# One projection in a two-block transformer kernel: its matmuls ordered by token block and not by column half, with the normalisation between them

## The chip, the core and the metric

The kernel runs on one core of one Trainium2 chip. The metric is the device time of one execution in microseconds (us), the median of three runs; lower is better.

## The reference, cut to what matters

The whole reference is two residual blocks (forgetting and dilated attention with retention after it, then a block of a state-space mixer beside sliding-window attention and a gated feed-forward part). x has 256 tokens (two blocks of 128) and 1024 channels. The change touches the seam of the second block between its mixing and its feed-forward part:

```
merged = concatenate([rms_norm(y_ssm, g_ssm_out), rms_norm(y_attn, g_attn_out)])   # 256 x (512 + 512)
h  = h + rms_norm(merged @ w_out, g_post_mix)                                      # 256 x 1024
hn = rms_norm(h, g_pre_ffn)
gu = hn @ w_gate_up                                                                # 256 x 5632
ff = (silu(gu[..., :D_FF]) * gu[..., D_FF:]) @ w_down
```

## The kernel before, in words

Each engine has a program of its own, written out in order by hand, and they meet at semaphores. TensorE multiplies in three passes per weight tile (high part of the activation by high part of the weight, low by high, high by low). Activations go to it transposed, in `act_t`: eight tiles of high parts (`x_hi`) and eight of low parts (`x_lo`).

Weights pass through a ring of four slots (`RING = 4`) in units of 128 x 1024 values (512 KB). SP loads a unit into `stage` once the low part of the unit four before it has been made; ScalarE makes the high part `w_hi` (line 627) once TensorE has used the unit four before it (`unit_used`); VectorE makes `w_lo` (line 914). `split_hi(u)` and `split_lo(u)` do this for all units below u that aren't done yet; `ahead(name)` does it to three units past the named chunk.

A chunk is 512 output columns. Its result lies in two PSUM banks, one for each token block; chunks alternate between banks 0, 1 and banks 2, 3. `start_chunk(name)` makes TensorE wait until the chunk before last, which used the same banks, has been drained; the semaphores are counted for even and odd chunks. In number, the chunks around the change are mix_attn 0 (35), glu 1 (36), glu 0 (37), mix_attn 1 (38), mix_ssm 0 (39), mix_ssm 1 (40), ffn 0 (41). I call the four units of mix_ssm U0, U1 (columns 0 to 511) and U2, U3 (columns 512 to 1023), and those of ffn 0 U4 to U7, those of ffn 1 U8 to U11. mix_attn and mix_ssm are the halves of `merged @ w_out` for the attention and the state-space part. mix_attn 1 is drained by ScalarE in `take_attn_half(1)` (line 846, two copies from PSUM into `mixed`), which stands behind the split of the transposed `ssm_out` (line 654) and its squares (line 643).

TensorE after mix_attn 1: it transposes `ssm_out` (line 1440), multiplies mix_ssm 0 for both blocks (lines 1508 to 1516), then mix_ssm 1, all of block 0 first and then block 1 (lines 1882 to 1887), runs small matmuls on a matrix of ones that only keep it busy (`keep_busy`, line 1574), and transposes x block by block (line 1898). Then the feed-forward chunks begin (lines 1548 and 1552).

VectorE adds the PSUM result to `mixed` (`mix_sum(c, b)`, line 1351), ScalarE squares it (line 868), VectorE multiplies it with the gain in place (`mix_gain`, line 1356), sums the squares of a block (`mix_mean`, line 1362), GpSimd raises that to the power -1/2 (line 597), VectorE updates x (`x_add(c, b)`, line 1367). TensorE transposes x, ScalarE makes the high parts (line 654, from PSUM, 256 tokens at once), VectorE the low parts (line 951).

Of the kernel before, what the change touches and what calls it, by code (L numbers as in the profile page):

```python
# [26 lines left out]
P = 128  # L27
# [105 lines left out]
def build(nc, t):  # L133
# [4 lines left out]
    with ExitStack() as ctx:  # L138
# [122 lines left out]
        x_ready, h_ready, mix_gained = sem("x_ready"), sem("h_ready"), sem("mix_gained")  # L261
# [356 lines left out]
        def _(act):  # L618
# [11 lines left out]
            def ahead(name):  # L630
                split_hi(last_unit[name] + 1 + AHEAD)
# [228 lines left out]
            hi_of_turned(3 * KD + 20, 4, 4, COL_GSSM)  # L860
            squares(5, lambda b: ssm_out[:, b, :], lambda b: gate_z[:, b, :])
            take_attn_half(1)
            ahead(("mix_ssm", 0))
            for c in range(2):
                for b in range(NB):
                    act.wait_ge(mixed_ready, 2 * c + b + 1)
                    half = slice(c * 512, (c + 1) * 512)
                    nc.scalar.activation(junk[:, b, half], mixed[:, b, half], ACT.Square, scale=D**-0.5, accum_out=(sumsq, sumsq_b)[c][:, 12 + b:13 + b]).then_inc(squared, 1)
# [36 lines left out]
        def _(dve):  # L905
            next_unit = [0]

            def split_lo(until):

                for u in range(next_unit[0], min(until, n_units)):  # L910
                    if u in lower_by_pool:
                        continue
                    dve.wait_ge(hi_ready, u + 1)
                    nc.vector.tensor_tensor(w_lo[:, u % RING, :], stage[:, u % RING, :], w_hi[:, u % RING, :].bitcast(F32), ALU.subtract).then_inc(lo_ready, 1)  # L914
                next_unit[0] = max(next_unit[0], min(until, n_units))

            def ahead(name):
                split_lo(last_unit[name] + 1 + AHEAD)
# [430 lines left out]
            def mix_sum(c, b):  # L1349

                STT(mixed[:, b, halves[c]], result(("mix_ssm", c))[:, b, :], rstd[:, 10 + b:11 + b], mixed[:, b, halves[c]], ALU.mult, ALU.add).then_inc(mixed_ready, 1)

            def mix_gain(c, b):

                dve.wait_ge(squared, squared_count(5) + 2 * c + b + 1)
                return TT(mixed[:, b, halves[c]], mixed[:, b, halves[c]], row_a[:, halves[c]], ALU.mult)

            def mix_mean(b):

                dve.wait_ge(squared, squared_count(5) + 2 + b + 1)  # L1360
                c = slice(12 + b, 13 + b)
                STT(sumsq[:, c], sumsq[:, c], EPS, sumsq_b[:, c], ALU.add, ALU.add).then_inc(block_mean, 1)

            def x_add(c, b):

                dve.wait_ge(rstd_ready, 7 + b)
                STT(x[:, b, halves[c]], mixed[:, b, halves[c]], rstd[:, 12 + b:13 + b], x[:, b, halves[c]], ALU.mult, ALU.add).then_inc(x_ready, 1)

            ahead(("mix_ssm", 0))
            chunk_drained(dve, ("mix_attn", 0))  # L1370
            chunk_done(dve, ("mix_ssm", 0))
            for b in range(NB):
                mix_sum(0, b)
            mix_gain(0, 0)
            mix_gain(0, 1).then_inc(drain_sem(("mix_ssm", 0)), 1)
            chunk_drained(dve, ("mix_attn", 1))
            dve.wait_ge(mix_block, 1)
            mix_sum(1, 0)
            mix_gain(1, 0).then_inc(mix_gained, 1)
            mix_mean(0)  # L1380
            chunk_done(dve, ("mix_ssm", 1))
            mix_sum(1, 1)
            chunk_drained(dve, ("mix_ssm", 0))
            dve.wait_ge(mix_gained, 1)
            x_add(0, 0)
            mix_mean(1)
            x_add(1, 0)
            mix_gain(1, 1).then_inc(drain_sem(("mix_ssm", 1)), 1)
            chunk_drained(dve, ("mix_ssm", 1))
            x_add(0, 1)  # L1390
            x_add(1, 1)
            lo_of_turned(3 * KD + 24, 4, 0, COL_FFN, KD)
            split_lo(next_unit[0] + 1)
            lo_of_turned(3 * KD + 28, 4, 4, COL_FFN + 4, KD + 4)
# [37 lines left out]
        def _(pe):  # L1432
# [59 lines left out]
            def lower_there(name, j):  # L1492

                wait_lower(pe, chunks[name][0] + j)
# [74 lines left out]
            def after_lo(count):  # L1569
                return lambda k: pe.wait_ge(act_hi, count + k + 1), lambda k: pe.wait_ge(act_lo, count + k + 1)  # L1570
# [302 lines left out]
            name = ("mix_ssm", 1)  # L1873
            start_chunk(name)
            for b in range(NB):
                tok = slice(b * P, (b + 1) * P)
                out = result(name)[:, b, :]
                for j in range(2):
                    hi, lo = unit_of(name, j)
                    for i in range(2):  # L1880
                        k = 2 * j + i
                        mm(out, x_hi(4 + k)[:, tok], hi[:, i, :], start=(k == 0), stop=False)
                        mm(out, x_lo(4 + k)[:, tok], hi[:, i, :], start=False, stop=False)
                    lower_there(name, j)
                    for i in range(2):
                        k = 2 * j + i
                        ins = mm(out, x_hi(4 + k)[:, tok], lo[:, i, :], start=False, stop=(k == CT - 1))
                    if b == 1:
                        ins.then_inc(unit_used, 1)
                if b == 0:  # L1890
                    ins.then_inc(mix_block, 1)
            for b in range(NB):
                keep_busy((6, 3)[b], (7, 0)[b])
                for k in range(KD):
                    if k % 4 == 0:
                        pe.wait_ge(x_ready, 2 * b + k // 4 + 1)
                    o = 4 * BANK + k * S + b * P
                    ins = nc.tensor.transpose(ps[:, o:o + P], x[:, b, k * P:(k + 1) * P], ident[:])
                    if b == 1:
                        ins.then_inc(turned, 1)  # L1900
            for c in range(11):
                start_chunk(("ffn", c))
                if c == 0:
# [63 lines left out]
```

## Time and profile before

| | |
|---|---|
| median of 3 runs | 798.84 us (797.82 to 799.75) |
| profiled execution, its own time | 795.62 us |
| its span, first to last instruction | 793.8 us |
| TensorE busy | 776.1 us, 98% of the span |
| VectorE, ScalarE, GpSimd busy | 513.3, 405.3, 232.8 us |
| mean granted TensorE clock | 0.996 |
| moved by DMA | 130.72 MB, 165 GB/s |

Times below are microseconds from the start of the span. A row of the timeline gives the start and the length of a run of like instructions, the engine, the source line, what is written and read, the shape and the count; in brackets stands how long the engine sat idle before it, and what ended that. PEld is the weight load of TensorE, PE its matmul. The granted clock is given as a share of 2.4 GHz.

### The profile page before, as it was taken

To read this page: it belongs to the slowest core of one execution; us is meant where nothing else is said; L and a number is where in the kernel's file an instruction comes from. 1 tells how busy PE (TensorE), PEld (TensorE's weight loads), DVE (VectorE), ACT (ScalarE), POOL (GpSimd) and SP (SyncE) were. 2 spreads that over 40 slices of the span, in tenths; PEclk is the share of its full clock that TensorE was granted. 3 is DMA by queue.
4 is the path that set the end of the run, shared out by engine and by line. 5 is a ranking of instruction groups with operands and counts; after the bars stand their busy time and mean duration, and the time that the engine had idled before them with its cause. 6 is when DMAs were issued, how large, how long until landed. Compare 5 with 4: busy or idle time off the path is not lost.

```text
span 793.8 us, 12695 instructions
## 1 busy us (share of the span) xinstructions
PE 776.1 (98%) x5133; PEld 679.3 (86%) x5133; DVE 513.3 (65%) x753; ACT 405.3 (51%) x649; POOL 232.8 (29%) x186
## 2 busy tenths in 40 slices
PE   7999999999999999999999999998999999999996
PEld 6889988999888889987778888987887888888885
DVE  4756864764547657865557965766678776777453
ACT  5754436534565545344335545717766555556341
POOL 3031895570742000036009910126002111011010
PEclk9999999999999999999999999999999999999999
DMA  8997895387721554654545556430363656655651
GB/s 218 213 266 217 208 207 150 82 193 170 167 81 51 187 173 147 213 171 147 158 136 158 179 195 185 135 132 2 119 220 127 199 186 210 187 176 172 220 177 54
DMA packets 77821, 130.72 MB, mean 165 GB/s; under 512 B 4414, under 2 KB 28210, under 8 KB 77634
## 3 DMA queue, kind: packets, MB, share of 16 engines
q1 hardware_dynamic: 76418, 125.00, 54.4%
q0 software_dynamic: 1200, 4.83, 1.9%
q8 instruction: 41, 0.67, 0.3%
q14 instruction: 18, 0.15, 0.1%
q10 hardware_dynamic: 144, 0.07, 0.0%
HBM read 128.82 MB, written 1.06 MB: 164 GB/s over the span
## 4 chain that ended last, share of the span: by engine, by line
PE 94%; DVE 2%; ACT 2%; issue 1%; DMA 1%; POOL 0%; DVEq 0%; SPq 0%; POOLq 0%; ACTq 0%
PE ps L1508 15%; PE ps L1516 15%; PE ps L1512 15%; PE ps L1548 10%; PE ps L1527 6%; PE ps L1531 6%; PE ps L1535 6%; PE ps L1552 5%; PE ps L1615 2%; PE ps L1634 2%; PE ps L1647 1%; PE ps L1646 1%; PE ps L1645 1%; PE ps L1925 1%; PE ps L1790 1%
## 5 line engine op out<-in xcount | busy, mean ns | idle before, releaser
L914 DVE TENSOR_TENSOR w_lo<-stage,w_hi 128x1024 fp32r<-128x1024 f32 x226 | 296.1, 1329 | 164.8 <-ACT w_hi L627 164.4
L627 ACT ACTIVATE w_hi<-stage 128x1024 fp32r<-128x1024 f32 x232 | 242.5, 1061 | 237.1 <-PE ps L1516 116.8
L1508 PE MATMUL ps<-w_hi,act_t 128*128 128x512 f32 (+1 forms) x376 | 102.5, 396 | 3.1 <-issue 2.6
L1516 PE MATMUL ps<-w_lo,act_t 128*128 128x512 f32 (+1 forms) x376 | 99.6, 388 | 1.0 <-issue 1.0
L1548 PE MATMUL ps<-act_t,w_hi 128*128 128x512 f32 x352 | 88.3, 393 | 0.7 <-DVE act_t L951 0.7
L1508 PEld LDWEIGHTS ps<-w_hi,act_t 128*128 128x128 f32 x376 | 68.4, 189 | 18.5 <-issue 5.7
L1516 PEld LDWEIGHTS ps<-w_lo,act_t 128*128 128x128 f32 x376 | 70.2, 190 | 15.7 <-issue 1.2
L1512 PE MATMUL ps<-w_hi,act_t 128*128 128x512 f32 (+1 forms) x312 | 82.3, 387 | 0.0
L1548 PEld LDWEIGHTS ps<-act_t,w_hi 128*128 128x128 f32 x352 | 63.3, 189 | 12.1 <-issue 0.9
L1512 PEld LDWEIGHTS ps<-w_hi,act_t 128*128 128x128 f32 x312 | 58.0, 189 | 12.0
L1527 PE MATMUL ps<-act_t,w_hi 128*128 128x256 f32 x416 | 58.8, 284 | 0.0
L1531 PE MATMUL ps<-act_t,w_hi 128*128 128x256 f32 x416 | 58.4, 283 | 0.0
L1535 PE MATMUL ps<-act_t,w_lo 128*128 128x256 f32 x416 | 58.4, 283 | 0.0
L1527 PEld LDWEIGHTS ps<-act_t,w_hi 128*128 128x128 f32 x416 | 53.8, 193 | 0.2
L1535 PEld LDWEIGHTS ps<-act_t,w_lo 128*128 128x128 f32 x416 | 53.7, 193 | 0.0
L1531 PEld LDWEIGHTS ps<-act_t,w_hi 128*128 128x128 f32 x416 | 53.7, 193 | 0.0
L1552 PEld LDWEIGHTS ps<-act_t,w_lo 128*128 128x128 f32 x352 | 48.0, 190 | 3.4
L1552 PE MATMUL ps<-act_t,w_lo 128*128 128x256 f32 x352 | 49.1, 283 | 0.0
L604 POOL TENSOR_TENSOR big<-big 128x512 f32<-128x512 f32 x11 | 14.3, 1300 | 105.5 <-ACT big L884 105.5
L1512 PE MATMUL ps<-w_hi,y_lo 128*128 128x512 f32 x128 | 34.3, 390 | 0.0
L1512 PEld LDWEIGHTS ps<-w_hi,y_lo 128*128 128x128 f32 x128 | 24.1, 188 | 5.1
L433 POOL TENSOR_TENSOR sumsq<-sumsq,sumsq_b 128x2 f32<-128x2 f32 x2 | 0.4, 194 | 91.0 <-ACT junk L643 91.0
(364 smaller groups left out, 1195.4 us busy)
## 6 DMA issues: line engine op xcount, KB each, us to landing
stage<-in_even_w_in SPq DMA_DIRECT2D x64, 512.0 KB, 5.7
stage<-in_odd_w_in SPq DMA_DIRECT2D x48, 512.0 KB, 4.2
stage<-in_w_gate_up SPq DMA_DIRECT2D x44, 512.0 KB, 4.6
stage<-in_w_down SPq DMA_DIRECT2D x22, 512.0 KB, 4.5
stage<-in_even_w_out SPq DMA_DIRECT2D x16, 512.0 KB, 4.3
stage<-in_odd_w_out SPq DMA_DIRECT2D x16, 512.0 KB, 4.1
stage<-in_w_in SPq DMA_DIRECT2D x10, 512.0 KB, 3.7
stage<-in_w_out SPq DMA_DIRECT2D x8, 512.0 KB, 4.9
```

The costliest lines, as they stand in the source:

```text
L627: nc.scalar.activation(w_hi[:, u % RING, :], stage[:, u % RING, :], ACT.Copy).then_inc(hi_ready, 1)
L914: nc.vector.tensor_tensor(w_lo[:, u % RING, :], stage[:, u % RING, :], w_hi[:, u % RING, :].bitcast(F32), ALU.subtract).then_inc(lo_ready, 1)
L1508: mm(out[:, b, :], a_hi(k)[:, tok[b]], hi[:, i, :], start=(k == 0), stop=False)
L1512: mm(out[:, b, :], a_lo(k)[:, tok[b]], hi[:, i, :], start=False, stop=False)
L1516: ins = mm(out[:, b, :], a_hi(k)[:, tok[b]], lo[:, i, :], start=False, stop=(k == k_tiles - 1))
L1527: mm(out[m], columns(hi[:, i, :], m), act_t[:, k, :], start=(k == 0 and m % 2 == 0), stop=False, skip_group_check=True)
L1531: mm(out[m], columns(hi[:, i, :], m), act_t[:, KD + k, :], start=False, stop=False, skip_group_check=True)
L1535: ins = mm(out[m], columns(lo[:, i, :], m), act_t[:, k, :], start=False, stop=(k == k_tiles - 1), skip_group_check=True)
L1548: mm(out[m], hi[:, i, w[m]], both[:, :, k, :], start=(k == 0), stop=(k == KD - 1), skip_group_check=True)
L1552: ins = mm(out[m][:, 0, :], lo[:, i, w[m]], act_t[:, k, :], start=False, stop=(k == KD - 1), skip_group_check=True)
L1615: even = mm(bank(0, width, at), qs[0][:, tok], ks[0][:, 0:width], start=True, stop=True)
L1634: ins = nc.tensor.transpose(bank(2 + n % 2, P, part * P), prob[:, n % 3, part * P:(part + 1) * P], ident[:])
```

## The change

mix_ssm 0 and mix_ssm 1 are no longer one after the other. TensorE calls `start_chunk` for both, then multiplies block 0 with U0, U1, U2, U3, and then block 1 with the same four. Before the last unit of block 1 it transposes block 0 of x (`turn_block(0)`). The gained halves go into `ssm_out` and `gate_z` and not back into `mixed`, so `mix_gain` waits for the sum alone and not for the squares. ScalarE and VectorE make the high and low parts of x for one block at a time (128 tokens, eight tiles each), block 0 with semaphores of its own. The splits of the weight units U3 to U5 are given new places. `keep_busy` is called once, with 9 matmuls, before block 1 of x is transposed; before, it was called with 6 ahead of block 0 and with 3 ahead of block 1. (In the trace each of these matmuls leaves two records, so 6 of them are a row with x12.)

```diff
@@ scalar engine
-            ahead(("mix_ssm", 0))
-            for c in range(2):
-                for b in range(NB):
-                    act.wait_ge(mixed_ready, 2 * c + b + 1)
-                    ...
+            split_hi(last_unit[("mix_ssm", 1)] + 1)
+            def hi_of_block(b, made):
+                for k in range(KD):
+                    act.wait_ge(x_turned, KD * b + (k | 1) + 1)
+                    o = 4 * BANK + k * S + b * P
+                    nc.scalar.activation(act_t[:, k, b * P:(b + 1) * P], ps[:, o:o + P], ACT.Copy, scale=col[:, COL_FFN + k:COL_FFN + k + 1]).then_inc(made, 1)
+            mix_squares(0, 0)
+            mix_squares(1, 0)
+            mix_squares(0, 1)
+            split_hi(last_unit[("mix_ssm", 1)] + 3)
+            hi_of_block(0, first_hi)
+            mix_squares(1, 1)
+            hi_of_block(1, act_hi)
             ahead(("mix_ssm", 1))
-            hi_of_turned(3 * KD + 24, KD, 0, COL_FFN)
@@ vector engine
             def mix_gain(c, b):
-                dve.wait_ge(squared, squared_count(5) + 2 * c + b + 1)
-                return TT(mixed[:, b, halves[c]], mixed[:, b, halves[c]], row_a[:, halves[c]], ALU.mult)
+                dve.wait_ge(mixed_ready, 2 * b + c + 1)
+                TT(gained[c][:, b, :], mixed[:, b, halves[c]], row_a[:, halves[c]], ALU.mult).then_inc(drain_sem(("mix_ssm", c)) if b == 1 else mix_gained, 1)
...
+            split_lo(last_unit[("mix_ssm", 1)] + 1)
+            for c in range(2):
+                chunk_drained(dve, ("mix_attn", c))
+                dve.wait_ge(mix_block, c + 1)
+                mix_sum(c, 0)
+                mix_gain(c, 0)
+            mix_mean(0)
             chunk_done(dve, ("mix_ssm", 0))
...
+            mix_sum(0, 1)
+            mix_gain(0, 1)
+            x_add(0, 0)
+            x_add(1, 0)
+            split_lo(last_unit[("mix_ssm", 1)] + 2)
+            lo_of_block(0, first_hi, 0, first_lo)
             chunk_done(dve, ("mix_ssm", 1))
             mix_sum(1, 1)
...
+            mix_gain(1, 1)
             mix_mean(1)
...
+            split_lo(last_unit[("mix_ssm", 1)] + 3)
             x_add(0, 1)
             x_add(1, 1)
...
+            lo_of_block(1, act_hi, 3 * KD + 24, act_lo)
             split_lo(last_unit[("ffn", 0)] + 1)
@@ tensor engine
-            mix_part("mix_ssm", 0, 4, after_lo(3 * KD + 20))
...
+            for c in range(2):
+                start_chunk(("mix_ssm", c))
+            hi_there, lo_there = after_lo(3 * KD + 20)
+            for b in range(NB):
+                tok = slice(b * P, (b + 1) * P)
+                for c in range(2):
+                    name = ("mix_ssm", c)
+                    out = result(name)[:, b, :]
+                    for j in range(2):
...
+                        if b == 1:
+                            ins.then_inc(unit_used, 1)
+                        if (b, c, j) == (1, 1, 0):
+                            turn_block(0)
+                    if b == 0:
+                        ins.then_inc(mix_block, 1)
+            chunk_drained(pe, ("mix_ssm", 0))
+            keep_busy(9, number[("mix_ssm", 0)] % 2 * 2)
+            pe.wait_ge(first_lo, KD)
+            turn_block(1)
```

## Rows read from the trace of the kernel before

**Rows 1.** The page, part 1: busy time, share of the span, instructions.

```profile
PE 776.1 (98%) x5133; PEld 679.3 (86%) x5133; DVE 513.3 (65%) x753; ACT 405.3 (51%) x649; POOL 232.8 (29%) x186
```

**Rows 2.** Windows: PE, PEld, DVE, ACT, POOL busy, clock, DMA share, GB/s.

```profile
640.00:700.00 60.00, 60.00 (x347) 52.96 (x346) 43.45 (x44) 33.85 (x44) 7.80 (x6) 1.00 0.59 182
```

**Rows 3.** Timeline of TensorE around the two mix_ssm chunks.

```profile
585.59 1.03 PE L1440 MATMUL ps<-ident,ssm_out 128*128 128x128 f32 x8
...
586.84 1.16 PE L1508 MATMUL ps<-w_hi,act_t 128*128 128x512 f32 x4 [0.22 <-ACT act_t L654]
...
597.36 0.62 PE L1887 MATMUL ps<-w_lo,act_t 128*128 128x512 f32 x2
597.82 1.50 PE L1574 MATMUL ps<-ones 128*128 128x128 f32 x12
600.22 1.39 PE L1898 MATMUL ps<-ident,x 128*128 128x128 f32 x8 [0.91 <-DVE x L1367]
...
602.34 1.32 PE L1898 MATMUL ps<-ident,x 128*128 128x128 f32 x8
604.32 2.08 PE L1548 MATMUL ps<-act_t,w_hi 128*128 128x512 f32 x8 [0.66 <-DVE act_t L951]
```

**Rows 4.** Timeline of VectorE, ScalarE and GpSimd, 598 to 604 us.

```profile
598.54 0.74 DVE L1351 SCALAR_TENSOR_TENSOR mixed<-ps,rstd,mixed 128x512 f32<-128x512 f32 x1
...
599.32 0.63 ACT L868 ACTIVATE junk<-mixed 128x512 f32<-128x512 f32 x1 [1.49 <-DVE mixed L1351]
...
600.08 0.15 DVE L1362 SCALAR_TENSOR_TENSOR sumsq<-sumsq,sumsq_b 128x1 f32<-128x1 f32 x1
...
600.32 0.99 POOL L597 TENSOR_TENSOR rstd<-sumsq,neg_half 128x1 f32<-128x1 f32 x1 [1.03 <-DVE sumsq L1362]
600.82 0.68 DVE L1356 TENSOR_TENSOR mixed<-mixed,row_a 128x512 f32<-128x512 f32 x1
...
601.53 1.42 DVE L1367 SCALAR_TENSOR_TENSOR x<-mixed,rstd,x 128x512 f32<-128x512 f32 x2
...
602.82 3.03 ACT L654 ACTIVATE act_t<-ps,col 128x256 fp32r<-128x256 f32 x8 [0.88 <-PE ps L1898]
...
603.69 1.66 DVE L951 SCALAR_TENSOR_TENSOR act_t<-ps,col,act_t 128x256 fp32r<-128x256 f32 x4 [0.74 <-ACT act_t L654]
```

**Rows 5.** Timeline of ScalarE, 586 to 590 us.

```profile
586.22 1.57 ACT L654 ACTIVATE act_t<-ps,col 128x256 fp32r<-128x256 f32 x4 [2.04 <-PE ps L1440]
587.66 0.65 ACT L643 ACTIVATE gate_z<-ssm_out 128x512 f32<-128x512 f32 x1
...
588.89 1.27 ACT L846 ACTIVATE mixed<-ps,rstd 128x512 f32<-128x512 f32 x2
```

**Rows 6.** Groups by line, shapes apart: busy us, mean ns of one.

```profile
L818 ACT ACTIVATE qkv<-ps,rstd_in 128x128 f32<-128x128 f32 x2 | 0.7, 368 | 0.0
```

**Rows 7.** Timeline of GpSimd and VectorE: short GpSimd operations and weight splits.

```profile
589.09 0.19 POOL L434 TENSOR_SCALAR rstd<-sumsq 128x2 f32<-128x2 f32 x1 [22.14 <-ACT gate_z L643]
...
598.71 0.57 POOL L597 TENSOR_TENSOR rstd<-sumsq,neg_half 128x1 f32<-128x1 f32 x1 [8.08 <-DVE sumsq L1362]
...
607.97 2.35 DVE L914 TENSOR_TENSOR w_lo<-stage,w_hi 128x1024 fp32r<-128x1024 f32 x2
608.01 2.36 POOL L434 TENSOR_SCALAR rstd<-sumsq 128x2 f32<-128x2 f32 x1 [6.70 <-ACT junk L643]
```

**Rows 8.** Timeline of TensorE at the start of the kernel.

```profile
11.09 1.17 PE L1508 MATMUL ps<-w_hi,act_t 128*128 128x512 f32 x4 [2.63 <-issue]
...
17.33 1.07 PE L1516 MATMUL ps<-w_lo,act_t 128*128 128x512 f32 x4
```

**Rows 9.** Windows there, columns as in rows 2.

```profile
12.00:13.00 1.00, 1.00 (x5) 0.76 (x4) 1.00 (x4) 1.00 (x3) 0.00 (x0) 0.61 0.71 274
...
14.00:15.00 1.00, 1.00 (x4) 0.71 (x4) 1.00 (x4) 1.00 (x3) 0.00 (x0) 0.50 1.01 205
15.00:16.00 1.00, 1.00 (x5) 0.82 (x4) 1.00 (x3) 1.00 (x4) 0.00 (x0) 0.69 1.13 207
```

**Rows 10.** The page, part 6: DMA issues, KB each, us to landing.

```profile
stage<-in_w_gate_up SPq DMA_DIRECT2D x44, 512.0 KB, 4.6
```

More of the change, by code:

```diff
@@ L260, in build @@
         turned, act_hi, act_lo = sem("turned"), sem("act_hi"), sem("act_lo")
-        x_ready, h_ready, mix_gained = sem("x_ready"), sem("h_ready"), sem("mix_gained")
+        x_ready, x_turned, h_ready, mix_gained, first_hi, first_lo = (sem(n) for n in ("x_ready", "x_turned", "h_ready", "mix_gained", "first_hi", "first_lo"))
         dve_step, act_step, pool_step = sem("dve_step"), sem("act_step"), sem("pool_step")
@@ L862, in _, with mix_squares @@
             take_attn_half(1)
-            ahead(("mix_ssm", 0))
-            for c in range(2):
-                for b in range(NB):
-                    act.wait_ge(mixed_ready, 2 * c + b + 1)
-                    half = slice(c * 512, (c + 1) * 512)
-                    nc.scalar.activation(junk[:, b, half], mixed[:, b, half], ACT.Square, scale=D**-0.5, accum_out=(sumsq, sumsq_b)[c][:, 12 + b:13 + b]).then_inc(squared, 1)
+            split_hi(last_unit[("mix_ssm", 1)] + 1)
+            def mix_squares(c, b):
+                act.wait_ge(mixed_ready, 2 * b + c + 1)
+                half = slice(c * 512, (c + 1) * 512)
+                nc.scalar.activation(junk[:, b, half], mixed[:, b, half], ACT.Square, scale=D**-0.5, accum_out=(sumsq, sumsq_b)[c][:, 12 + b:13 + b]).then_inc(squared, 1)
+            def hi_of_block(b, made):
[10 more added lines that the diff above has]
+            hi_of_block(1, act_hi)
             ahead(("mix_ssm", 1))
-            hi_of_turned(3 * KD + 24, KD, 0, COL_FFN)
             act.wait_ge(x_ready, 2 * NB)
@@ L1351, in mix_sum @@
                 STT(mixed[:, b, halves[c]], result(("mix_ssm", c))[:, b, :], rstd[:, 10 + b:11 + b], mixed[:, b, halves[c]], ALU.mult, ALU.add).then_inc(mixed_ready, 1)
+            gained = (ssm_out, gate_z)
             def mix_gain(c, b):
-                dve.wait_ge(squared, squared_count(5) + 2 * c + b + 1)
-                return TT(mixed[:, b, halves[c]], mixed[:, b, halves[c]], row_a[:, halves[c]], ALU.mult)
+                dve.wait_ge(mixed_ready, 2 * b + c + 1)
+                TT(gained[c][:, b, :], mixed[:, b, halves[c]], row_a[:, halves[c]], ALU.mult).then_inc(drain_sem(("mix_ssm", c)) if b == 1 else mix_gained, 1)
             def mix_mean(b):
-                dve.wait_ge(squared, squared_count(5) + 2 + b + 1)
+                dve.wait_ge(squared, squared_count(5) + 2 * b + 2)
                 c = slice(12 + b, 13 + b)
@@ L1366, in x_add @@
                 dve.wait_ge(rstd_ready, 7 + b)
-                STT(x[:, b, halves[c]], mixed[:, b, halves[c]], rstd[:, 12 + b:13 + b], x[:, b, halves[c]], ALU.mult, ALU.add).then_inc(x_ready, 1)
-            ahead(("mix_ssm", 0))
-            chunk_drained(dve, ("mix_attn", 0))
-            chunk_done(dve, ("mix_ssm", 0))
[L1372 to L1380, printed above, removed]
+                if b == 1:
+                    chunk_drained(dve, ("mix_ssm", c))
+                else:
+                    dve.wait_ge(mix_gained, c + 1)
+                STT(x[:, b, halves[c]], gained[c][:, b, :], rstd[:, 12 + b:13 + b], x[:, b, halves[c]], ALU.mult, ALU.add).then_inc(x_ready, 1)
+            def lo_of_block(b, hi_made, n_hi, made):
+                for k in range(KD):
+                    dve.wait_ge(hi_made, n_hi + (k | 1) + 1)
+                    o, tok = 4 * BANK + k * S + b * P, slice(b * P, (b + 1) * P)
+                    STT(act_t[:, KD + k, tok], ps[:, o:o + P], col[:, COL_FFN + k:COL_FFN + k + 1], act_t[:, k, tok].bitcast(F32), ALU.mult, ALU.subtract).then_inc(made, 1)
@@ L1381, in _ @@
             chunk_done(dve, ("mix_ssm", 1))
             mix_sum(1, 1)
-            chunk_drained(dve, ("mix_ssm", 0))
-            dve.wait_ge(mix_gained, 1)
-            x_add(0, 0)
+            mix_gain(1, 1)
             mix_mean(1)
-            x_add(1, 0)
-            mix_gain(1, 1).then_inc(drain_sem(("mix_ssm", 1)), 1)
-            chunk_drained(dve, ("mix_ssm", 1))
+            split_lo(last_unit[("mix_ssm", 1)] + 3)
             x_add(0, 1)
             x_add(1, 1)
-            lo_of_turned(3 * KD + 24, 4, 0, COL_FFN, KD)
@@ L1393, in _ @@
-            split_lo(next_unit[0] + 1)
-            lo_of_turned(3 * KD + 28, 4, 4, COL_FFN + 4, KD + 4)
+            lo_of_block(1, act_hi, 3 * KD + 24, act_lo)
             split_lo(last_unit[("ffn", 0)] + 1)
@@ L1871, in _, with turn_block @@
             turn_rows(lambda b, k: ssm_out[:, b, k * P:(k + 1) * P], 4, 4)
-            mix_part("mix_ssm", 0, 4, after_lo(3 * KD + 20))
[L1873 to L1893, printed above, removed]
+            def turn_block(b):
                 for k in range(KD):
@@ L1897, in _ @@
                     o = 4 * BANK + k * S + b * P
-                    ins = nc.tensor.transpose(ps[:, o:o + P], x[:, b, k * P:(k + 1) * P], ident[:])
-                    if b == 1:
-                        ins.then_inc(turned, 1)
+                    nc.tensor.transpose(ps[:, o:o + P], x[:, b, k * P:(k + 1) * P], ident[:]).then_inc(x_turned, 1)
+            for c in range(2):
[7 more added lines that the diff above has]
+                    for j in range(2):
+                        hi, lo = unit_of(name, j)
+                        for k in range(2 * j, 2 * j + 2):
+                            hi_there(k)
+                            mm(out, x_hi(4 + k)[:, tok], hi[:, k % 2, :], start=(k == 0), stop=False)
+                        for k in range(2 * j, 2 * j + 2):
+                            lo_there(k)
+                            mm(out, x_lo(4 + k)[:, tok], hi[:, k % 2, :], start=False, stop=False)
+                        lower_there(name, j)
+                        for k in range(2 * j, 2 * j + 2):
+                            ins = mm(out, x_hi(4 + k)[:, tok], lo[:, k % 2, :], start=False, stop=(k == CT - 1))
+                        if b == 1:
+                            ins.then_inc(unit_used, 1)
[7 more added lines that the diff above has]
+            turn_block(1)
             for c in range(11):
```

## The prediction

> **What bounds the kernel now.** I read the page first: TensorE is busy for 776.1 of 793.8 us [rows 1], so only its order and its waits can matter. The windows say how strictly: from 640 to 700 us it is busy 60.00 of 60.00 us, at clock 1.00 [rows 2]. Whatever delays the first feed-forward matmul delays the end by as much; no slack behind it could swallow a loss. The question is thus when that matmul (line 1548) starts: at 604.32 us now [rows 3].
>
> The timeline of TensorE gives the seam. The matmuls of mix_ssm start at 586.84 and end at 597.36 + 0.62 = 597.98 [rows 3]. They are 48, and the last pair is issued by about 597.6, so they run one per 0.227 us. From 597.98 to 604.32, 6.34 us, TensorE does only transposes and matmuls on ones [rows 3]. What sets this tail is the dependent chain on the other engines [rows 4]: sum 598.54, square 599.32, mean 600.08, power 600.32 to 601.31, `x_add` 601.53, transposes 602.34, high parts 602.82, low parts 603.69, matmul 604.32. The change wants most of block 0's part of this to lie beside the matmuls.
>
> **The wait that the new order puts in front.** I go through the edit with the before trace as time axis; nothing changes up to the transposes of `ssm_out` (585.59 to 586.62 [rows 3]). Now `start_chunk` of mix_ssm 1 (number 40) stands ahead of all of the 48 matmuls. It waits until all even chunks before it, mix_attn 1 (38) among them, have been drained. That is ScalarE's work at line 846: 588.89 + 1.27 = 590.16 [rows 5], behind four high parts (586.22) and the two squares (from 587.66). ScalarE's order up to there is not edited. Before, TensorE reached this wait after the 24 matmuls of mix_ssm 0, 586.84 + 24 x 0.227 = 592.3, when it was long over: those matmuls were its cover, and the cover is gone. Queued behind the wait are all 48 matmuls, and all of VectorE's sums. First matmul: 590.16 plus the 0.14 us that lies between 604.18, the end of the first low part, and 604.32 [rows 3, 4] (low part taken as 0.49), so 590.3. **Cost 3.45 us.** It is read from code and two rows, so I give it 0.3 us of play.
>
> **Block 0.** Matmuls 1 to 12 are issued by 593.0, 24 by 595.7. Its column 0 is summed under the matmuls. Column 1: the last matmul is over at 595.9, sum to 596.65, square and its read to 597.4 (0.76 us from start of square to start of mean, 599.32 to 600.08 [rows 4]), mean 597.45, power 597.7 to 598.25 (0.57 with VectorE quiet [rows 7]). But VectorE works in order, and ahead of `x_add(0, 0)` stand `mix_sum(0, 1)` and `mix_gain(0, 1)`. The sum waits for U1 used by block 1: 36 matmuls, 590.3 + 35 x 0.227 + 0.39 (the length of one, 0.62 for two less 0.23) = 598.6. Then sum 598.65 to 599.4, gain (0.68) to 600.1, two `x_add` at 0.75 and spacing 0.67 [rows 4], ready at 600.85 and 601.5. TensorE has issued its 42 matmuls at 599.8 and waits for block 0 until 600.9, transposes four tiles, waits again until 601.55, transposes four, and goes on at 602.05. Eight transposes without a wait take about 1.0 us (1.03 [rows 3]); here they take 2.25, **1.25 us of it waiting, 1.0 work** that before lay in the tail. The last six matmuls end at 603.6. That is 597.98 + 3.45 + 2.25, or 603.65.
>
> **Block 1, the new tail.** ScalarE squares `mixed(0, 1)` by 600.2, splits U4 and U5 (about 1.0 us each, the weight copies are on its queue now ahead of the activations) to 602.2, and starts on the high parts of block 0. A 128 x 128 copy from PSUM takes 0.368 [rows 6]; eight of 128 x 256 take 3.03, 0.37 apart [rows 4]. 128 tokens fewer save some 0.10 each (bounds: 0.37, no saving, and half, 0.19); I take 0.27, so the last is done at 604.4. VectorE splits U4 (1.2) from 601.45 to 602.65, then follows ScalarE's pairs; a low part of 256 costs 0.39 apiece (1.66 for four), half as wide I take 0.26. Last low part of block 0 at 605.0. Only behind it stands `mix_sum(1, 1)`, though its matmuls ended at 603.6: **1.35 us of queueing**. From there: sum 605.0 to 605.75, square, mean at 606.5, power issued at 606.7.
>
> Behind the mean, VectorE splits U5, 606.6 to 607.8 (1.2, half of 2.35 [rows 7]), and `x_add(0, 1)` stands behind that. If the power were done in 0.57 to 0.99 [rows 4, 7] the split would just cover it: `x_add` at 607.75. But the power starts inside the split. In rows 7 a GpSimd operation that takes 0.19 elsewhere takes 2.36 us, 608.01 to 610.37, when two splits run on VectorE from 607.97 to 610.32: it ends as they do. So I let the power run after the split, 607.8 + 0.57, and `x_add(0, 1)` at 608.4. The Trainium skill, SBUF — State Buffer, "SBUF: two separate sides", states this as a rule: GpSimd and VectorE share a pair of ports, an instruction of VectorE with two inputs in SBUF holds it for its whole length, and the other blocks fully. By that rule the sum is +6.5, without it +5.9; the trace's 2.36 us agrees with it.
>
> `x_add(0, 1)` to first matmul: before 604.32 - 601.53 = 2.79 [rows 4]; half-wide tiles save two times 0.1 on ScalarE and 0.13 on VectorE, so 2.4. **First feed-forward matmul at 610.8, against 604.32: +6.5 us.** The nine matmuls on ones take 2.2 us (1.50 for six [rows 3]) from 603.5 and are over at 605.7, well before block 1; they cost nothing. Block 1's later tiles arrive 0.3 us apart against 0.46 us for two matmuls, no cost. The ring: U8 is now loaded when U4's low part is done (602.65) and lands in 4.6 us [rows 10], at 607.3; it is needed four units after 610.8, each longer than its eight 512-wide matmuls at 0.227, so not before 618.1. U9, loaded at 607.8, lands at 612.4. No cost. The reciprocal row for the feed-forward part needs squares of x, which follow U6's split: some 3.6 us from first matmul to squares done before, about the same now, and the row is used after three units. No cost, up to 0.4 if it is late.
>
> **The clock.** At the start of the kernel TensorE idles 2.63 us before 11.09 [rows 8], and then the granted clock goes to 0.61, 0.50, and back through 0.69 in the sixteenth us [rows 9]: from the level of 2.4 GHz to that of 1.2 and back. The 24 matmuls from 11.09 to the four at 17.33 show the price: 20 issued in 6.24 us, not 20 x 0.227 = 4.54, a loss of 1.7. In the changed kernel the wait in front is 3.5 us of idling (586.8 to 590.3), longer than that one, and the second, from 605.7 to the transposes at 609.1, 3.4 us, is too. Before, the longest hole here is 0.91 [rows 3]. So I expect a slow stretch twice. How much of it lies on matmuls depends on where it falls: between 0 and 1.7 each; I take 1.3 for the first (all of block 0 hangs on those matmuls) and 0.9 for the second (transposes and waits take part of it). **+2.2 us.** The Trainium skill, TensorE: Matmul & The Clock Gate, "What's actually happening", says that the throttled state is the default and that activity releases it; rows 9 agree.
>
> **Sum**: 3.45 (front) + 2.25 (block 0 in the stream) + 0.8 (tail: 610.8 - 603.65 = 7.15 against 6.34) = 6.5, + 2.2 clock = **+8.7 us**. The profiled execution would be 795.62 + 8.7 = 804.3; the median of the runs shown is 798.84, so 807.5.
>
> **The rivals.**
> - Forecast, both holes lower the clock: 0.50. +7.5 to +10.
> - No slow stretch, or only one: the clock survives, because the hole is bracketed by dense matmuls or falls luckily. For it: holes of 1 us change nothing here. Against it: 2.63 us sufficed once. +6.5, or +7.5 to +8 with one: 0.38.
> - The front wait is hidden: ScalarE drains mix_attn 1 before TensorE asks. It would take the two copies 3.45 us earlier, ahead of the squares and parts. +3.0, and with the clock of the second hole +4: 0.04.
> - The other side, faster: TensorE finds every semaphore of the seam raised, the overlap as drawn. It decides only if the banks are free by 586.8 and x of block 0 by the time of the 42nd matmul. Then 48 matmuls (10.9) and eight transposes (1.0) end at 598.8, and the shortest tail is sum 0.75, square to mean 0.76, mean and power 0.8, `x_add` to matmul 2.4, with gaps 4.9: 603.7, **-0.6 us**, 798.2. Against it: 590.16 [rows 5]. 0.03.
> - The tail is worse than counted (a late row, GpSimd held longer, a slow stretch twice as long as at the start): +10 to +12.5: 0.05.
>
> **How the numbers follow.** Measurements of this kernel tell about 0.2%, 1.6 us, from no change. All cases but the fourth are slower by more than that: slower 0.95; -0.6 us counts as same, and something that I don't see could add to it: same 0.03, faster 0.02. Range: down to +5.2, the case without slow stretches with 1.3 us less in my queueing sums (front 0.3, tile widths 0.4, power not held 0.6), 804.0; up to +12.2: two whole slow stretches (3.4), the late row (0.4), the same 1.3 of queueing sums on the other side, and the power held 0.6 longer, 811.0.
>
> **What would show it.** In the changed profile: TensorE idle 3.5 us before the first mix_ssm matmul, released by ScalarE line 846; a wait of about 1.1 us for `x_add` before block 0's transposes; `mix_sum(1, 1)` starting right after the eighth low part of block 0; the second power over 1 us long and ending after U5's split; clock below 1.00 near 590 to 594 and 609 to 614; the first feed-forward matmul 6.5 to 9 us later in the span, and all later stages as long as before. I am wrong if the front wait is short, if the clock stays at 1.00 (then +6.5), or if the feed-forward part holds slack after all.

## The result: 8 us slower, and the profile after

| | before | changed |
|---|---|---|
| median | 798.64 us (4 runs, 797.82 to 799.75) | 806.66 us (4 runs, 806.02 to 808.36) |
| ratio | | 1.0123, 95% interval 1.0097 to 1.0149 |
| profiled execution, span, mean clock | 795.62, 793.8, 0.996 | 808.36, 806.6, 0.989 |

807.5 was forecast, in a range of 804.0 to 811.0. The two spans differ by 12.8 us, more than the medians. 3.9 us of that arose before the edit: the transposes of `ssm_out` start at 585.59 [rows 3] before and at 589.44 after, and the timeline of the changed kernel's TensorE shows where: a wait of 4.05 us at 59 us, with slow matmuls behind it, which the profiled execution of the kernel before did not have. It ends when VectorE has made the low part of the forget-gate weights, which stands behind the split of a weight unit that came late from DMA. The edit doesn't touch this part, and waits of 1.3 to 4.3 us stand there in all but one of the profiles below. (The kernel before varied from 794.3 to 803.0 us over the runs of this study, so single executions differ by that much without an edit.) I therefore count every time from the start of those transposes, called T0.

Timeline of TensorE in the changed kernel, which answers to rows 3:

```profile
59.24 0.58 PE L1620 MATMUL ps<-act_t,wf_hi 128*128 128x256 f32 x1 [4.05 <-DVE wf_lo L1057]
...
589.44 1.03 PE L1464 MATMUL ps<-ident,ssm_out 128*128 128x128 f32 x8
594.11 0.89 PE L1916 MATMUL ps<-w_hi,act_t 128*128 128x512 f32 x2 [3.64 <-ACT mixed L846]
...
604.87 0.61 PE L1922 MATMUL ps<-w_lo,act_t 128*128 128x512 f32 x2
606.36 1.32 PE L1902 MATMUL ps<-ident,x 128*128 128x128 f32 x8 [0.87 <-DVE x L1388]
...
608.45 0.62 PE L1922 MATMUL ps<-w_lo,act_t 128*128 128x512 f32 x2
608.91 2.17 PE L1598 MATMUL ps<-ones 128*128 128x128 f32 x18
614.36 1.68 PE L1902 MATMUL ps<-ident,x 128*128 128x128 f32 x8 [3.29 <-DVE x L1388]
615.97 3.20 PE L1572 MATMUL ps<-act_t,w_hi 128*128 128x512 f32 x8
```

Read the brackets: 3.64 us of idling in front, ended by ScalarE's copy out of mix_attn 1's banks (line 846), 0.87 for x of block 0, 3.29 for x of block 1. T0 to the first feed-forward matmul is 615.97 - 589.44 = 26.53 us, against 604.32 - 585.59 = 18.73: +7.8. Its first eight matmuls then take 3.20 us and not 2.08 [rows 3]: +1.1. The windows show the clock:

```profile
592.00:594.00 2.00, 0.00 (x0) 0.00 (x0) 0.60 (x2) 2.00 (x7) 0.97 (x3) 1.00 0.77 264
594.00:596.00 2.00, 1.89 (x5) 1.59 (x6) 0.91 (x1) 0.96 (x2) 0.48 (x1) 0.61 0.40 102
596.00:598.00 2.00, 2.00 (x6) 1.55 (x5) 0.31 (x1) 0.00 (x0) 0.00 (x0) 0.53 0.72 215
...
614.00:616.00 2.00, 1.64 (x9) 1.20 (x9) 1.41 (x5) 1.19 (x5) 0.00 (x0) 0.73 0.77 260
616.00:618.00 2.00, 2.00 (x6) 1.63 (x6) 1.67 (x8) 2.00 (x6) 0.00 (x0) 0.50 0.01 3
...
640.00:700.00 60.00, 60.00 (x344) 52.72 (x343) 43.42 (x45) 34.91 (x45) 7.81 (x6) 1.00 0.61 188
```

The clock is the third number from the right: 0.50 is the level of 1.2 GHz. After each long hole the clock falls to it and comes back; in the first hole (592 to 594 us) it was still 1.00. From 640 to 700 us TensorE is busy without a gap, as in rows 2, and the 3.85 us from before T0 and the 8.90 us of the seam (table below) together are the whole difference of the spans, so the seam's loss goes through to the end.

Timelines of VectorE and GpSimd in the changed kernel, which answer to rows 4 and 7:

```profile
604.16 0.75 DVE L1366 SCALAR_TENSOR_TENSOR mixed<-ps,rstd,mixed 128x512 f32<-128x512 f32 x1 [0.95 <-PE ps L1922]
...
608.11 2.16 DVE L1395 SCALAR_TENSOR_TENSOR act_t<-ps,col,act_t 128x128 fp32r<-128x128 f32 x8
610.19 0.74 DVE L1366 SCALAR_TENSOR_TENSOR mixed<-ps,rstd,mixed 128x512 f32<-128x512 f32 x1
...
611.80 1.22 DVE L929 TENSOR_TENSOR w_lo<-stage,w_hi 128x1024 fp32r<-128x1024 f32 x1
613.47 0.75 DVE L1388 SCALAR_TENSOR_TENSOR x<-ssm_out,rstd,x 128x512 f32<-128x512 f32 x1 [0.45 <-POOL rstd L597]
```

```profile
603.30 0.57 POOL L597 TENSOR_TENSOR rstd<-sumsq,neg_half 128x1 f32<-128x1 f32 x1 [8.82 <-DVE sumsq L1379]
611.96 1.47 POOL L597 TENSOR_TENSOR rstd<-sumsq,neg_half 128x1 f32<-128x1 f32 x1 [8.09 <-DVE sumsq L1379]
```

The last `mix_sum` starts at 610.19, right behind the eighth low part of block 0, though its matmuls were over at 609.07. The second power takes 1.47 us, and begins 0.16 us into U5's split.

### The profile page after: what moved, and what is told of

Same layout as the page of the kernel before. It is cut to its first block, busy times and chain, and to the rows that moved or that the text cites. A ratio compares the mean times of both kernels' runs of the same rounds, so it can differ in the third digit from the quotient of the medians.

```text
span 806.6 us, 12720 instructions
## 1 busy us (share of the span) xinstructions
PE 782.3 (97%) x5133; PEld 684.6 (85%) x5133; DVE 515.1 (64%) x761; ACT 406.6 (50%) x657; POOL 230.8 (29%) x186
## 4 chain that ended last, share of the span: by engine, by line
PE 89%; DMA 4%; DVE 3%; ACT 3%; issue 1%; POOL 0%; SPq 0%; DVEq 0%; POOLq 0%; ACTq 0%
PE ps L1532 13%; PE ps L1540 13%; PE ps L1536 13%; PE ps L1572 10%; PE ps L1551 6%; PE ps L1555 6%; PE ps L1559 6%; PE ps L1576 5%; DMA stage<-in_even_w_in 4%; PE ps L1639 2%; PE ps L1658 2%; PE ps L1671 1%; PE ps L1670 1%; PE ps L1669 1%; PE ps L1957 1%; ACT w_hi L627 1%
## 5 line engine op out<-in xcount | busy, mean ns | idle before, releaser
L1532 PE MATMUL ps<-w_hi,act_t 128*128 128x512 f32 (+1 forms) x368 | 100.2, 395 | 0.5 <-ACT act_t L654 0.3
L1540 PE MATMUL ps<-w_lo,act_t 128*128 128x512 f32 (+1 forms) x368 | 96.6, 385 | 0.0
L1540 PEld LDWEIGHTS ps<-w_lo,act_t 128*128 128x128 f32 x368 | 68.1, 188 | 14.1
L1532 PEld LDWEIGHTS ps<-w_hi,act_t 128*128 128x128 f32 x368 | 66.6, 188 | 15.5 <-issue 3.0
L1536 PE MATMUL ps<-w_hi,act_t 128*128 128x512 f32 (+1 forms) x304 | 79.4, 384 | 0.0
L1536 PEld LDWEIGHTS ps<-w_hi,act_t 128*128 128x128 f32 x304 | 56.1, 188 | 11.6
```

Source lines behind the costliest of these rows:

```text
L1532: mm(out[:, b, :], a_hi(k)[:, tok[b]], hi[:, i, :], start=(k == 0), stop=False)
L1536: mm(out[:, b, :], a_lo(k)[:, tok[b]], hi[:, i, :], start=False, stop=False)
L1540: ins = mm(out[:, b, :], a_hi(k)[:, tok[b]], lo[:, i, :], start=False, stop=(k == k_tiles - 1))
```

## The experiments

All kernels start from the changed one and carry one or two edits, the mended ones several. Times are medians; "seam" is T0 to the start of the second feed-forward unit in the profiled execution, which holds both the waits and the slow matmuls of the first unit (before: 607.19 - 585.59 = 21.60 us).

| kernel | median, us | ratio to before, 95% interval | T0 to first feed-forward matmul | seam, over before |
|---|---|---|---|---|
| changed | 806.66 | 1.0123 (1.0097 to 1.0149) | 26.53 | 30.50, +8.9 |
| changed, run again | 807.93 | 1.0122 (1.0097 to 1.0146) | 27.71 | 32.11, +10.5 |
| bank wait late | 803.98 | 1.0076 (1.0052 to 1.0100) | 22.25 | 26.11, +4.5 |
| front hole filled | 805.86 | 1.0103 (1.0079 to 1.0128) | 24.93 | 29.37, +7.8 |
| second hole filled | 805.19 | 1.0096 (1.0074 to 1.0118) | 27.72 | 30.59, +9.0 |
| both filled | 804.18 | 1.0081 (1.0057 to 1.0105) | 24.92 | 27.80, +6.2 |
| U5's low part later | 806.74 | 1.0111 (1.0087 to 1.0135) | 26.63 | 29.50, +7.9 |
| x of block 0 first | 809.55 | 1.0152 (1.0125 to 1.0179) | 27.84 | 32.56, +11.0 |
| x first, copies early | 806.98 | 1.0114 (1.0088 to 1.0141) | 26.47 | 30.95, +9.4 |
| mended | 800.85 | 1.0035 (1.0014 to 1.0056) | 20.21 | 24.38, +2.8 |
| mended, filled | 799.37 | 1.0019 (0.9996 to 1.0041) | 19.92 | 22.80, +1.2 |

The seam's excess and the medians' excess over 798.0 to 798.6 agree within 1.5 us in most rows and within 2.1 in all, so the seam holds the cause, and nothing ahead of T0 adds to the medians. The intervals are some 2 us wide to each side; steps of less than that are judged by the trace, of which there is one for each kernel.

**The changed kernel again.**

> The changed kernel itself, as a yardstick for the runs beside it. Both theories: +8 us against the kernel before (between +7 and +9.5), with a hole of about 3.6 us ahead of the first mix_ssm matmul, one of about 3.3 us ahead of block 1's transposes, and slow matmuls behind each.

The holes are there, 3.64 and 3.29 us, with slow matmuls behind each; the medians differ by 9.7 us, just above the expected range. Timeline and one window of its TensorE:

```profile
588.72 1.19 PE L1916 MATMUL ps<-w_hi,act_t 128*128 128x512 f32 x2 [3.64 <-ACT mixed L846]
...
602.14 1.32 PE L1902 MATMUL ps<-ident,x 128*128 128x128 f32 x8 [0.87 <-DVE x L1388]
...
611.75 3.61 PE L1572 MATMUL ps<-act_t,w_hi 128*128 128x512 f32 x8 [0.38 <-DVE act_t L1395]
```

```profile
588.00:590.00 2.00, 1.28 (x3) 1.13 (x4) 0.30 (x1) 1.56 (x3) 1.09 (x2) 0.50 0.39 119
```

Its slow stretch at the front was the longer one: from the first mix_ssm matmul to the transposes of x it takes 602.14 - 588.72 = 13.42 us, against 606.36 - 594.11 = 12.25 in the first profile. Here the clock was at 0.50 when the matmuls began; in the first profile it fell behind the first of them.

**Bank wait late.**

```diff
-            for c in range(2):
-                start_chunk(("mix_ssm", c))
+            start_chunk(("mix_ssm", 0))
...
                     name = ("mix_ssm", c)
+                    if (b, c) == (0, 1):
+                        start_chunk(name)
```

> TensorE asks for the banks of mix_ssm 1 only before it first writes them, 12 matmuls later. My theory (the bank wait in front costs 3.45 us, and the hole it leaves costs up to 1.7 more through the clock): hole 3.6 us gone, a wait of about 0.7 us behind the 12th matmul in its place, no slow stretch at the front; 4 to 5 us faster than the changed kernel, +3 to +4 over the one before. Rival (the loss sits in the queueing on VectorE and in the tail, the front hole only moves a wait that would come at block 0's x anyway): less than 2 us faster than the changed kernel.

The hole of 3.64 us is gone. Timeline of its TensorE:

```profile
588.44 1.03 PE L1464 MATMUL ps<-ident,ssm_out 128*128 128x128 f32 x8
589.70 0.77 PE L1917 MATMUL ps<-w_hi,act_t 128*128 128x512 f32 x2 [0.22 <-ACT act_t L654]
...
601.08 1.32 PE L1902 MATMUL ps<-ident,x 128*128 128x128 f32 x8 [0.87 <-DVE x L1388]
...
609.08 1.69 PE L1902 MATMUL ps<-ident,x 128*128 128x128 f32 x8 [3.29 <-DVE x L1388]
610.69 3.07 PE L1572 MATMUL ps<-act_t,w_hi 128*128 128x512 f32 x8
```

T0 to first feed-forward matmul falls by 4.3 us against the first profile of the changed kernel, 5.5 against the second; the medians by 2.7 and 4.0. That is less than the 4 to 5 us expected, and +5.7 us over the kernel before, not +3 to +4. The kernel with both holes filled, below, has this wait and no slow clock, and its first feed-forward matmul comes 24.92 us after T0: against it the late bank wait gives 2.7 us. The first mix_ssm matmul comes 3.4 us earlier, and 0.7 us are lost again among the next ones, mostly to waits for low parts. The rest of the gain is the slow clock at the front. The slow stretch behind the second hole is still there. The later bank wait is hardly visible, since the first matmuls wait a little for low parts. What the rival held, that a front wait only moves to block 0's x, is wrong: the wait there is 0.87 us as before, so the whole chain moved with the front.

**Front hole filled, second hole filled, both filled.** Order and waits stay; TensorE does matmuls on ones while it waits.

```diff
             start_chunk(("mix_ssm", 0))
+            keep_busy(13, number[("mix_ssm", 0)] % 2 * 2)
             start_chunk(("mix_ssm", 1))
...
-            keep_busy(9, number[("mix_ssm", 0)] % 2 * 2)
+            keep_busy(20, number[("mix_ssm", 0)] % 2 * 2)
```

> Between the two bank waits stand 13 matmuls on ones (26 records, about 3.2 us), the order and the wait stay. My theory (the front hole lowers the clock): slow stretch at the front gone, matmuls there 0.227 us apart, 1.3 to 1.7 us faster than the changed kernel. Rival (the slow stretch has nothing to do with the hole, or its loss is absorbed by the wait for block 0's x): same time as the changed kernel within 0.5 us.

> keep_busy of 20 and not 9 ahead of block 1's transposes, which fills the second hole (3.3 us) to some 0.6 us. My theory: slow stretch behind the first feed-forward matmul gone, 0.7 to 1.5 us faster than the changed kernel. Rival (that hole is harmless on average, since transposes and waits take the slow stretch): within 0.5 us of the changed kernel.

> The changed kernel with both holes filled with matmuls on ones (13 in front, 20 and not 9 at the second). My theory: no slow stretch in the seam; what is left against the kernel before is waiting and queueing alone, +5.5 to +6.5 us, so 2 to 3.5 us faster than the changed kernel. Rival (the clock costs little): +7.5 us or more.

Timeline of TensorE with both filled:

```profile
588.50 3.07 PE L1598 MATMUL ps<-ones 128*128 128x128 f32 x26
592.25 0.73 PE L1917 MATMUL ps<-w_hi,act_t 128*128 128x512 f32 x2 [0.69 <-ACT mixed L846]
...
602.94 1.32 PE L1902 MATMUL ps<-ident,x 128*128 128x128 f32 x8 [0.88 <-DVE x L1388]
605.48 4.62 PE L1598 MATMUL ps<-ones 128*128 128x128 f32 x40
610.94 1.23 PE L1902 MATMUL ps<-ident,x 128*128 128x128 f32 x8 [0.83 <-DVE x L1388]
612.54 2.08 PE L1572 MATMUL ps<-act_t,w_hi 128*128 128x512 f32 x8 [0.37 <-DVE act_t L1395]
```

The first matmul of mix_ssm comes 4.63 us after T0 (592.25 - 587.62), as late as in the changed kernel (4.67): nothing about the wait has changed. But from there to the transposes of x it is 10.69 us, not 12.25 or 13.42: the slow clock cost 1.6 and 2.7 us in those two executions. The first feed-forward unit takes 2.08 for its eight wide matmuls, not 3.20. Both filled: 2.5 to 3.7 us faster than the changed kernel by the medians, as expected. The front alone gave 0.8 to 2.1 us by the medians, the second hole alone 1.5 to 2.7. In the traces each filling took away its own slow stretch and left the other: with the front filled 10.69 us (603.95 - 593.26) and then 3.57 for the eight wide matmuls, with the second filled 13.43 (603.05 - 589.62) and then 2.08. What stays, 6.2 us in seam and median alike, is waiting and queueing. The two holes' effect on the clock is shown: filling them left the order and the waits as they were.

**U5's low part later.** Without this call, U5's low part is made by the next `split_lo`, behind block 1's low parts.

```diff
             mix_mean(1)
-            split_lo(last_unit[("mix_ssm", 1)] + 3)
             x_add(0, 1)
             x_add(1, 1)
             lo_of_block(1, act_hi, 3 * KD + 24, act_lo)
```

> Against the changed kernel only the low part of unit U5 moves on VectorE, from behind the mean of block 1 to behind the low parts of block 1. My theory (GpSimd's power of block 1 is held by that split, which has two inputs in SBUF): the second power takes 0.57 to 0.7 us and not 1.47, the x update of block 1 starts 0.8 to 0.9 us earlier, 0.7 to 0.9 us faster than the changed kernel, in the trace of the seam if not beyond the spread of the times. Rival (the power is long for another reason, as that it runs right behind an idle spell, and only the split in front of the x update counts): the power stays at 1.47 and the update starts at the power's end as before.

GpSimd's row is what it was made for:

```profile
602.10 0.57 POOL L597 TENSOR_TENSOR rstd<-sumsq,neg_half 128x1 f32<-128x1 f32 x1 [9.83 <-DVE sumsq L1379]
610.76 0.55 POOL L597 TENSOR_TENSOR rstd<-sumsq,neg_half 128x1 f32<-128x1 f32 x1 [8.09 <-DVE sumsq L1379]
```

0.55 and not 1.47, with the same idle spell of 8.09 us in front, so the rival falls. Mean to x update: 611.35 - 610.52 = 0.83 us, against 613.47 - 611.72 = 1.75. T0 to first feed-forward matmul is 1.1 us less than in the kernel run again: these 0.9 us, and 0.2 from a slightly shorter first stretch (13.25 us). The second hole shrank to 2.38 us, and in this profile no slow stretch stands behind it. In the medians, 1.2 us under the kernel run again and 0.1 above the first series, the gain is within the spread.

**x of block 0 first.**

```diff
+            x_add(0, 0)
+            x_add(1, 0)
             chunk_done(dve, ("mix_ssm", 0))
             mix_sum(0, 1)
             mix_gain(0, 1)
-            x_add(0, 0)
-            x_add(1, 0)
```

> Against the changed kernel the two x updates of block 0 stand ahead of the sum and the gain of column half 0 of block 1 on VectorE. My theory (the wait of TensorE ahead of block 0's transposes is queueing on VectorE, not the length of block 0's chain): hole of 0.87 us and the second small one gone, last mix_ssm matmul some 1.1 us earlier; 0.8 to 1.2 us faster than the changed kernel. Rival (the chain of block 0 itself, power included, ends too late): hole stays over 0.5 us.

A miss: the hole went away, and the kernel got slower. Timelines of its TensorE, ScalarE and VectorE:

```profile
587.56 1.03 PE L1464 MATMUL ps<-ident,ssm_out 128*128 128x128 f32 x8
...
601.62 0.62 PE L1922 MATMUL ps<-w_lo,act_t 128*128 128x512 f32 x2
...
603.44 1.04 PE L1902 MATMUL ps<-ident,x 128*128 128x128 f32 x8
...
613.55 1.94 PE L1902 MATMUL ps<-ident,x 128*128 128x128 f32 x8 [5.67 <-DVE x L1388]
```

```profile
604.77 1.99 ACT L627 ACTIVATE w_hi<-stage 128x1024 fp32r<-128x1024 f32 x2
606.66 2.16 ACT L876 ACTIVATE act_t<-ps,col 128x128 fp32r<-128x128 f32 x8
```

```profile
605.84 1.23 DVE L929 TENSOR_TENSOR w_lo<-stage,w_hi 128x1024 fp32r<-128x1024 f32 x1 [1.01 <-ACT w_hi L627]
607.30 2.16 DVE L1395 SCALAR_TENSOR_TENSOR act_t<-ps,col,act_t 128x128 fp32r<-128x128 f32 x8 [0.23 <-ACT act_t L876]
609.38 0.74 DVE L1366 SCALAR_TENSOR_TENSOR mixed<-ps,rstd,mixed 128x512 f32<-128x512 f32 x1
```

TensorE is through with block 0's transposes at 604.5, but the third square came 1.1 us later (its sum now stands behind the x updates), ScalarE's two weight copies behind it too, and then VectorE idles 1.01 us for U4's high part. The last sum starts 609.38 - 587.56 = 21.82 us after T0, against 20.75 (610.19 - 589.44) in the changed kernel's first profile. The changed kernel run again has 21.93, so the slow stretch in front has to be left out of the count. From the end of block 1's matmuls on U1, which the first of block 1's two sums waits for (602.24 here), to the last sum it is 7.14 us, against 6.06 in both profiles of the changed kernel (610.19 - 604.13 in the first). The second hole grew from 3.29 to 5.67 us, 1.3 by TensorE being done earlier and 1.1 by the later sum, and the slow stretch behind it grew too. So TensorE's wait at block 0's transposes was slack, not a price. New theory: from U1's matmuls to the last sum the queues of VectorE and ScalarE are the bound.

**x first, copies early.**

```diff
+            split_hi(last_unit[("mix_ssm", 1)] + 3)
             mix_squares(0, 1)
-            split_hi(last_unit[("mix_ssm", 1)] + 3)
```

> The x updates of block 0 first, as in the run that came out slower, and ScalarE's two weight copies (U4, U5) ahead of its third square and not behind it. New theory (between U1's use and the last sum the bound is the queue work: some 6 us of VectorE, and behind the third square 2 us of copies and 2.2 us of high parts on ScalarE; the wait of TensorE there is slack): the last sum starts 1.2 to 1.4 us earlier than with the x updates first alone, and only 0.2 to 0.4 us earlier than in the changed kernel, counted from the transposes of ssm_out; time 1.5 to 2.5 us under x first alone, within 1 us of the changed kernel. Rival (the copies have nothing to do with it): last sum as with x first alone.

The last sum starts at 607.49 - 587.04 = 20.45 us after T0, 1.4 less than with x first alone and 0.3 less than in the changed kernel's first profile, which had a slow stretch in front of the same length; from the end of block 1's matmuls on U1 it is 5.70 us, against 7.14 and 6.06; the median is 2.6 under the one and within 1 us of the other. The theory holds. From the first x update (601.57) to the last sum (607.49) VectorE has no idle time in its timeline: two x updates, a sum, a gain, U4's low part, eight low parts, 5.9 us. In the changed kernel the same work lies in 6.03 us (604.16 to 610.19), in another order.

**Mended, and mended with the hole filled.** Late bank wait; ScalarE drains mix_attn 1 ahead of the squares of `ssm_out`; x first, copies early; and VectorE's end of the seam as below. The first has 13 matmuls on ones, the second 17.

```diff
-            lo_of_block(0, first_hi, 0, first_lo)
             chunk_done(dve, ("mix_ssm", 1))
             mix_sum(1, 1)
-            mix_gain(1, 1)
+            lo_of_block(0, first_hi, 0, first_lo, range(4))
             mix_mean(1)
-            split_lo(last_unit[("mix_ssm", 1)] + 3)
+            lo_of_block(0, first_hi, 0, first_lo, range(4, 8))
             x_add(0, 1)
+            mix_gain(1, 1)
             x_add(1, 1)
```

> All the waits found are taken out of the changed kernel at once: late bank wait, ScalarE drains mix_attn 1 ahead of the squares, U4 and U5 split on ScalarE ahead of the third square, x updates of block 0 first, mix_sum of block 1 ahead of block 0's low parts, U5's low part later, 13 matmuls on ones. My theory (the new order has little to win: the tail is a chain of latencies that half a block shortens by about 1 us, and the transposes of block 0 put 1.0 us back into the stream): first feed-forward matmul 19 to 20 us after the ssm_out transposes start, against 18.73 before; time of the kernel before within +0 to +1.5 us, no slow stretch. Rival (the order is good and only its queueing was bad): under 18 us, and 1 to 2 us faster than the kernel before.

> The mended kernel with 17 and not 13 matmuls on ones, so that TensorE idles less than 0.3 us ahead of block 1's transposes. Theory: no slow stretch behind it, first unit of the feed-forward part 2.0 to 2.1 us and not 3.4, first matmul 19.8 to 20.2 us after the transposes of ssm_out start; 1 to 1.5 us faster than the mended kernel, +1 to +1.8 over the kernel before. Rival (the slow stretch comes all the same, since matmuls on ones and transposes are weak work for the clock): time as the mended kernel.

Timelines of TensorE, of the first and of the second:

```profile
607.53 0.63 PE L1902 MATMUL ps<-ident,x 128*128 128x128 f32 x4 [1.13 <-DVE x L1388]
608.90 1.06 PE L1902 MATMUL ps<-ident,x 128*128 128x128 f32 x4 [0.74 <-DVE x L1388]
609.61 3.38 PE L1572 MATMUL ps<-act_t,w_hi 128*128 128x512 f32 x8
```

```profile
589.49 1.03 PE L1464 MATMUL ps<-ident,ssm_out 128*128 128x128 f32 x8
...
601.16 1.05 PE L1902 MATMUL ps<-ident,x 128*128 128x128 f32 x8
...
602.98 0.62 PE L1923 MATMUL ps<-w_lo,act_t 128*128 128x512 f32 x2
603.44 3.96 PE L1598 MATMUL ps<-ones 128*128 128x128 f32 x34
607.63 0.63 PE L1902 MATMUL ps<-ident,x 128*128 128x128 f32 x4 [0.24 <-DVE x L1388]
609.00 0.66 PE L1902 MATMUL ps<-ident,x 128*128 128x128 f32 x4 [0.74 <-DVE x L1388]
609.41 2.09 PE L1572 MATMUL ps<-act_t,w_hi 128*128 128x512 f32 x8
```

First feed-forward matmul 20.21 and 19.92 us after T0, where 19 to 20 and 19.8 to 20.2 were expected, and no slow stretch in the second (2.09). In the first I had expected none and there was one: 3.38 us for the eight wide matmuls, behind holes of 1.13 and 0.74 us, and the kernel is 2.9 us slower than the one before, where at most 1.5 was expected. The second is 1.5 us faster than the first, as expected, and not to be told from the kernel before (1.0019, 0.9996 to 1.0041). No version beat the kernel before. The stream ends later: the last mix_ssm matmul is over 14.1 us after T0 (603.6), against 12.4 (597.98 - 585.59), by the eight transposes (0.8 to 1.0) and by first matmuls that wait for low parts. The tail from there is 609.41 - 603.6 = 5.8 us, against 6.34. So the work moved out of the tail saves 0.5 us there and the stream is 1.7 us longer, which is the 1.2 us that stay in the seam.

## Why the prediction was right, by its own steps

- **The front wait, 3.45 us, hit.** T0 to the first matmul was forecast as 590.3 - 585.59 = 4.71 and measured as 4.67; released by line 846. Taking it away gave more than any other single edit, though without its clock share it gave 2.7 us and not 3.45, since the first matmuls then wait for low parts.
- **Block 0 in the stream, 2.25 us: seen, but not a price.** TensorE loses 607.43 - 605.32 = 2.1 us there (605.32 is 604.87 and two matmuls at 0.227), as forecast. But the sum took these 2.25 as one of three terms that add up, and the runs with x first show that the 1.1 us of waiting in it buys nothing. The right step was the other one in the same text: the last sum stands behind VectorE's queue, forecast at 605.0 - 585.59 = 19.4 after T0 without slow clock, measured at 20.75 with 1.6 of it, so 19.1; with both holes filled it is 19.15. As that queue was walked through in full, the total came out right.
- **The tail: mis-sized by little.** From the last mix_ssm matmul to the first feed-forward one 7.15 was forecast, 615.97 - 609.07 = 6.9 measured. The power held by the split was right: forecast end at the split's end plus 0.57, measured 613.43, 0.41 behind the split's 613.02. Moving the split brought the x update 0.92 us forward; the 0.6 us of the forecast was the part of the hold alone, with the split still ahead of the update. The rule behind it (the Trainium skill, SBUF — State Buffer, "SBUF: two separate sides") is that a VectorE instruction with two inputs in SBUF has the port pair that it shares with GpSimd for its whole length, and GpSimd is shut out until then. The runs agree, 1.47 us beside the split and 0.55 without it; that ports are the reason is the skill's statement, and no run here separates it from another cause tied to the split.
- **The clock, 2.2 us: right in kind, the first term too small.** 1.3 was taken for the first hole and 0.9 for the second, with 1.7 as the most for each; measured were 1.6 and 1.1 in one execution, 2.7 and 1.5 in the next. The bound of 1.7 came from one slow stretch at the start of the kernel and did not hold for the first hole.
- **Sum.** 6.5 without the clock; both filled measured 6.2. With it 8.7; seam 8.9 and 10.5, medians +8.0 and +9.7. How close the first profile came is partly luck: the clock was 0.5 too low and the waiting 0.3 too high, and the second profile is 1.8 above.
- **Rivals.** Front wait hidden: no, 3.64 us. No slow stretch: not in the changed kernel, whose two profiles have both. The faster side was argued from a first feed-forward matmul at 603.7, which is 18.1 us after T0; the mended kernels got to 19.9 with VectorE's queue in the way. That -0.6 us is within reach was only argued, and no run bears it out.

## What to carry to other kernels

When a loop order is turned inside out, look first at which wait moves ahead of work that used to cover it: here a bank wait for a neighbour's drain passed 24 matmuls and became 3.6 us of idling. Before an engine's visible wait is called a price, walk the other engines' queues to the next common point; here 1.1 us of waiting was slack, and taking it away lengthened the queue that mattered. And a hole in TensorE's work has to be counted with the matmuls behind it: 3.6 and 3.3 us of idling brought 2.7 to 4.2 us more, which matmuls on ones in the same place took away.

## What was not expected of the hardware

- Short holes can be enough. In the mended kernel idle times of 1.13 and 0.74 us, with transposes between, were followed by a granted clock of 0.75 and 0.50 (608 to 610 and 610 to 612 us); with U5's low part later a hole of 2.38 us had none behind it, and its eight wide matmuls took 2.08 us. These runs don't say what decides.
- The loss behind the same hole came in two sizes. In six profiles the front hole is there and unfilled. In three of them (the changed kernel run again, second hole filled, U5's low part later) the granted clock fell to 0.50 inside the hole, 0.9 to 1.2 us ahead of the first mix_ssm matmul, and 2.6 to 2.7 us were lost; in the other three it fell between 0.1 us ahead of that matmul and 1.4 us behind it, and 1.5 to 1.6 us were lost. The spread of a kernel with such holes may come from this in part; that isn't shown, and the medians of the changed kernel's two series differ by 1.3 us.
- GpSimd's power takes 0.55 to 0.57 us in the seam with VectorE quiet or at low parts from PSUM, and 1.47 in all eight profiles with U5's split beside it, where it ends 0.41 us behind the split. The 0.99 us of rows 4 look the same: that power ends at 601.31, 0.42 us behind an x update that ran from 600.15 to 600.89.
